# Rows of per-token scales from a repeated statistics column times the identity, in place of a row of ones times a diagonal built on VectorE (a two-block transformer kernel, one Trainium2 core)

## The reference, cut to what matters

```
def rmsnorm_2(x, g):            # mean over the features of one token
    x * rsqrt(mean(x * x, -1) + 1e-6) * g

x = x + parallel_mixer(rmsnorm_2(x, norm_mix_g), ...)
    # inside: q_a = rmsnorm_2(c_q) @ w_uq;  kv = rmsnorm_2(c_kv) @ w_ukv
    #         norms of q_nope, q_rope, k_nope for each of 4 heads, of k_rope once
x = x + memory_cross_attention(rmsnorm_2(x, norm_x_g), ...)
    # inside: norms of q and k for each of 4 heads
x = x + square(relu(rmsnorm_2(x, norm_ffn_g) @ w_ff1)) @ w_ff2
```

## Time and profile before

| | us |
|---|---|
| median of three runs | 2190.63 |
| lowest, highest | 2187.43, 2197.18 |
| the profiled execution | 2182.91 |
| its span, first to last instruction | 2181.2 |
| PE busy | 2037.4 (93%) |
| POOL busy | 1546.2 (71%) |
| DVE busy | 903.0 (41%) |
| ACT busy | 648.0 (30%) |
| mean granted clock of TensorE | 0.962 of full |

### The profile page before, as it was taken

How to read it: one execution, slowest core, us unless ns; L and a number is a source line. 1 busy time by engine, 2 the same in 40 slices (tenths; PEclk the granted TensorE clock), 3 DMA queues, 4 the chain that set the end, 5 groups by cost and what they waited for, 6 DMA issues and landing times.

```text
span 2181.2 us, 26391 instructions
## 1 busy us (share of the span) xinstructions
PE 2037.4 (93%) x9749; PEld 1625.4 (75%) x9749; DVE 903.0 (41%) x1708; ACT 648.0 (30%) x1208; POOL 1546.2 (71%) x1379
## 2 busy tenths in 40 slices
PE   6999999999999999979999997888798989999998
PEld 4888888877766667758888885866466867888887
DVE  4566666631013334355104316854645056401421
ACT  3466666551034461122002102342231132200200
POOL 6799988887644347778889877633518908988984
PEclk9999999999989999989999998988798989999999
DMA  6212211123312122313322331111102302332332
GB/s 209 78 58 61 75 59 58 59 63 111 111 46 58 54 62 78 116 59 96 97 90 91 96 99 41 46 62 58 39 1 66 109 20 78 96 96 82 98 97 72
DMA packets 212122, 165.97 MB, mean 76 GB/s; under 512 B 13439, under 2 KB 208322, under 8 KB 211635
## 3 DMA queue, kind: packets, MB, share of 16 engines
q1 hardware_dynamic: 207126, 147.61, 22.6%
q10 hardware_dynamic: 4892, 17.01, 2.3%
HBM read 161.43 MB, written 7.37 MB: 77 GB/s over the span
## 4 chain that ended last, share of the span: by engine, by line
PE 79%; POOL 10%; DVE 7%; issue 2%; ACT 2%; DMA 0%; DVEq 0%; SPq 0%; ACTq 0%; POOLq 0%
PE bank L394 59%; POOL w_lo L2519 4%; PE bank L414 4%; PE bank L1315 3%; POOL w_hi L2514 3%; PE bank L1339 2%; PE bank L1325 2%; PE bank L2075 1%; POOL x_features L652 1%; PE bank L2084 1%; POOL arena L1032 1%; PE bank L1014 1%; DVE arena L1757 1%; PE bank L992 1%; PE bank L460 1%
## 5 line engine op out<-in xcount | busy, mean ns | idle before, releaser
L2514 POOL TENSOR_TENSOR w_hi<-w_raw,one 128x512 fp32r<-128x512 f32 (+2 forms) x520 | 529.4, 1048 | 561.1 <-PE bank L394 497.0
L2519 POOL TENSOR_TENSOR w_lo<-w_raw,w_hi 128x512 fp32r<-128x512 f32 (+2 forms) x600 | 745.5, 1273 | 34.7 <-ACT w_hi L1177 30.3
L394 PE MATMUL bank<-h_hi,w_hi 128*128 128x512 f32 (+1 forms) x1144 | 461.0, 403 | 38.3 <-DVE h_lo L623 15.2
L394 PE MATMUL bank<-h_hi,w_lo 128*128 128x512 f32 (+1 forms) x1144 | 446.8, 391 | 0.0
L394 PE MATMUL bank<-h_lo,w_hi 128*128 128x512 f32 (+1 forms) x1144 | 446.3, 390 | 0.0
L394 PE MATMUL bank<-a_hi,w_hi 128*128 128x512 f32 x896 | 358.1, 400 | 11.9 <-POOL w_lo L2519 7.4
L394 PE MATMUL bank<-a_lo,w_hi 128*128 128x512 f32 x896 | 357.2, 399 | 0.0
L394 PE MATMUL bank<-a_hi,w_lo 128*128 128x512 f32 x896 | 356.7, 398 | 0.0
L394 PEld LDWEIGHTS bank<-h_hi,w_hi 128*128 128x128 f32 x1144 | 220.3, 193 | 97.0 <-issue 19.8
L394 PEld LDWEIGHTS bank<-h_hi,w_lo 128*128 128x128 f32 x1144 | 220.0, 192 | 44.9
L394 PEld LDWEIGHTS bank<-h_lo,w_hi 128*128 128x128 f32 x1144 | 220.8, 193 | 38.7 <-issue 0.2
(11 more groups left out here) (379 smaller groups left out, 2732.1 us busy)
## 6 DMA issues: line engine op xcount, KB each, us to landing
w_raw<-in_w_in SPq DMA_DIRECT2D x32, 1024.0 KB, 5.2
w_raw<-in_w_ff SPq DMA_DIRECT2D x32, 1024.0 KB, 5.5
w_raw<-in_w_mlp_in SPq DMA_DIRECT2D x16, 1024.0 KB, 5.3
w_raw<-in_w_mlp_out SPq DMA_DIRECT2D x16, 1024.0 KB, 5.9
w_raw<-in_w_in SPq DMA_DIRECT2D x25, 512.0 KB, 4.1
w_raw<-in_w_ssd_out SPq DMA_DIRECT2D x8, 1024.0 KB, 5.8
bias_rows<-bias_row ACTq DMA_DIRECT2D x1, 4096.0 KB, 16.0
w_raw<-in_w_attn_out SPq DMA_DIRECT2D x4, 1024.0 KB, 5.2
```

The lines of the kernel that those rows point to most:

```text
L394: mm = pe.matmul(bank[:, 0:ntok], a, b[:, koff + k, 0:ntok], start=(k == 0 and n == 0), stop=(k == L.kb - 1 and n == 2))
L2514: pool.tensor_tensor(w_hi[:, slot, part], raw[:, slot, part], one[:].broadcast_to([P, n]), ALU.mult).then_inc(split_hi, 1)
L2519: ins = pool.tensor_tensor(w_lo[:, slot, part], raw[:, slot, part], w_hi[:, slot, part].bitcast(F32), ALU.subtract)
```

## The change

The diagonal is no longer made. The stationary operand of the row product becomes one column of the statistics table, repeated 128 times by a zero step; the moving operand becomes the identity. One such product yields the row of one tile of 128 tokens, so a row of 512 tokens takes four products, each with a stationary operand of its own, where there was one product with 512 columns. PE now waits for the reciprocal (`nx_inverse`, `la["inverse"]`). The ring of two diagonal buffers and DVE's wait for it are gone; the ring of three PSUM banks stays. `nstat` and `lstat` hold the same numbers as before.

```diff
         def root_row_pe(pe):
-            pe.wait_ge(nx_diag, nx_n["sum"])
-            pe.matmul(NROW[:], ones[:], NROOT, start=True, stop=True).then_inc(nx_row, 1)
+            pe.wait_ge(nx_inverse, nx_n["sum"])
+            for t in range(T):
+                mm = pe.matmul(NROW[:, t * P:(t + 1) * P], nstat[:, t:t + 1].broadcast_to([P, P]), ident[:], start=True, stop=True)
+            mm.then_inc(nx_row, 1)
...
             dve.wait_ge(nx_root, nx_n["rooted"])
-            dve_link(dve.reciprocal(nstat, nstat))
+            dve.reciprocal(nstat, nstat).then_inc(nx_inverse, 1)
             row_dve(dve)
...
         def row_dve(dve):
-            n = nx_n["acc"] // DB
-            dve.tensor_tensor(NROOT.rearrange("p (t f) -> p t f", t=T), ident[:].unsqueeze(1).broadcast_to([P, T, P]),
-                              nstat.unsqueeze(2).broadcast_to([P, T, P]), ALU.mult).then_inc(nx_diag, 1)
-            dve.wait_ge(nx_row, n)
+            dve.wait_ge(nx_row, nx_n["acc"] // DB)
...
         def rows_pe(pe, n, tiles=T):
 
-            pe.wait_ge(la["diag"], n + 1)
+            pe.wait_ge(la["inverse"], 1 if n == 0 else 2 if n < 3 else 3 if n < LATENT_ITEMS else 4)
             if n >= 3:
                 pe.wait_ge(la["out"], n - 2)
-            pe.matmul(ROW_RING[n % 3][:, 0:tiles * P], ones[:], DIAG[n % 2][:, 0:tiles * P], start=True, stop=True).then_inc(la["row"], 1)
-
-        def diag_dve(dve, n, col, tiles=T):
-            if n >= 2:
-                dve.wait_ge(la["row"], n - 1)
-            r = lstat[:, col:col + tiles].unsqueeze(2).broadcast_to([P, tiles, P])
-            dve.tensor_tensor(DIAG[n % 2][:, 0:tiles * P].rearrange("p (t f) -> p t f", t=tiles),
-                              ident[:].unsqueeze(1).broadcast_to([P, tiles, P]), r, ALU.mult).then_inc(la["diag"], 1)
+            col = 4 * n if n < LATENT_ITEMS else CROSS_ITEMS[n - LATENT_ITEMS][0]
+            for t in range(tiles):
+                mm = pe.matmul(ROW_RING[n % 3][:, t * P:(t + 1) * P], lstat[:, col + t:col + t + 1].broadcast_to([P, P]), ident[:],
+                               start=True, stop=True)
+            mm.then_inc(la["row"], 1)
...
         def norms_dve(dve, first, last):
             outs = norm_outputs()
-            diag_dve(dve, first, 4 * first)
             for n in range(first, last):
-                if n + 1 < last:
-                    diag_dve(dve, n + 1, 4 * (n + 1))
                 scale_dve(dve, n, *outs[n])
...
             dve.wait_ge(la["root"], 2)
-            dve_link(dve.reciprocal(lstat[:, 4:12], lstat[:, 4:12]))
+            dve.reciprocal(lstat[:, 4:12], lstat[:, 4:12]).then_inc(la["inverse"], 1)
             norms_dve(dve, 1, 3)
```

More of the change, by code:

```diff
@@ L526, in build_program @@
         nx_sq, nx_acc, nx_sum, nx_root, nx_hi, nx_lo, nx_add = (sem(f"nx_{k}") for k in ("sq", "acc", "sum", "root", "hi", "lo", "add"))
-        NSQ, NACC, NROOT = [A(8192, 512), A(8704, 512)], A(9216, 512), A(9728, 512)
-        nx_diag, nx_row, nx_post = sem("nx_diag"), sem("nx_row"), sem("nx_post")
+        NSQ, NACC = [A(8192, 512), A(8704, 512)], A(9216, 512)
+        nx_inverse, nx_row, nx_post = sem("nx_diag"), sem("nx_row"), sem("nx_post")
         nstat, NROW = small[:, 104:104 + T], banks[5]
@@ L2002, in build_program @@
         DIAG = [t[:, 15, :] for t in (a_free_hi, a_free_lo)]
-        la = {k: sem("la_" + k) for k in ("rope", "sw", "v", "vt", "vl", "ang", "sin", "sq", "ev", "sum", "root", "diag", "row", "out", "fin", "cos", "turned")}
+        la = {k: sem("la_" + k) for k in ("rope", "sw", "v", "vt", "vl", "ang", "sin", "sq", "ev", "sum", "root", "inverse", "row", "out", "fin", "cos", "turned")}
         RR = slice(64, 128)
@@ L2249, in latent_dve @@
             dve.wait_ge(la["root"], 1)
-            dve_link(dve.reciprocal(lstat[:, 0:4], lstat[:, 0:4]))
+            dve.reciprocal(lstat[:, 0:4], lstat[:, 0:4]).then_inc(la["inverse"], 1)
             norms_dve(dve, 0, 1)
@@ L2279, in latent_dve @@
             dve.wait_ge(la["root"], 3)
-            dve_link(dve.reciprocal(lstat[:, 12:60], lstat[:, 12:60]))
+            dve.reciprocal(lstat[:, 12:60], lstat[:, 12:60]).then_inc(la["inverse"], 1)
             norms_dve(dve, 3, 7)
@@ L2391, in cross_act @@
                 kvx_act(act, b)
-            act.wait_ge(nx_diag, nx_n["root"])
+            act.wait_ge(nx_inverse, nx_n["root"])
             for h in range(X_HEADS):
@@ L2415, in cross_dve @@
             dve.wait_ge(la["root"], 4)
-            dve_link(dve.reciprocal(lstat[:, 0:cross_cols], lstat[:, 0:cross_cols]))
+            dve.reciprocal(lstat[:, 0:cross_cols], lstat[:, 0:cross_cols]).then_inc(la["inverse"], 1)
             outs = [(XK[:, h, :], colv("xk")) for h in range(X_HEADS)] + [(XQ[:, h, :], colv("xq")) for h in range(X_HEADS)]
[L2418 to L2422, removed]
+            for i, out_ in enumerate(outs):
+                scale_dve(dve, LATENT_ITEMS + i, [out_], tiles=CROSS_ITEMS[i][1])
             dve.drain().then_inc(xa_q, 1)
```

## The result

The changed kernel takes 2170.76 us in the median of nine runs (2163.85 to 2176.89), the kernel before 2189.81 in nine (2181.13 to 2197.18). The ratio is 0.9919, with a 95% interval of 0.9899 to 0.9939: faster by 0.8%, which is 17.7 us (13.4 to 22.1); the medians lie 19.1 apart. The forecast was 25.5 us. The profiled execution took 2163.85 us with a span of 2162.1, against 2182.91 and 2181.2.

The account below looks back on a forecast made before the run. The chain lay 79% on TensorE, so DVE's diagonals counted only where it crossed them, in three stretches of the second block. Six terms summed to -25.5 us, from 2190.6 to 2165 us, range 2157 to 2182.

Parts of the forecast that it names:

- Items 1 and 2: Before latent block 4: both DVE diagonals go and the block starts earlier, -7.2 us.
- The clock behind it: Latent blocks 4 and 5 with their sums run at full clock instead of 1.2 GHz, -4.8 us.
- The rival by which the clock doesn't come back: PE's clock stays low in the latent blocks and items 3 to 14; sum about -16, 2174 us; chance 0.25.
- Items 3 to 14: Rows before the latent attention: PE sets the pace, POOL's rope is late next, first rope product comes earlier, -10.1 us.
- All of it reaches the end: From the latent attention on, POOL waits for PE before splitting, so the whole -25.5 us shortens the kernel.
- term 2: Latent blocks 4 and 5: PE's shorter idle time leaves its clock up, -4.8 us.
- Cross attention: 48 row passes after the cross reciprocal let the scores start earlier, -2.3 us.
- POOL's splits beside a diagonal: After the mixer, after the MLP and at `norm_x`, POOL's splits run faster without a diagonal beside them, -1.3 us.
- Rows between panels: Six rows, item 0 and five large norms, take 0.89 us instead of 0.86 each, +0.2 us.
- slower rival: Every row product pays its weight loads, 0.19 us on each pass; +15.7 us, 2206; chance 0.04.
- three signs of error: Passes of 0.2 us or more at full clock, latent blocks at 1.2 GHz, or the attention's first product waiting for POOL.
- term 3: Items 3 to 14 before the latent attention: first rope product at 1572.8 instead of 1582.89, -10.1 us.

Follow-up runs that it names:

- e1: Kernel before with the new rows for items 1 and 2 alone; ratio 0.9942, 11.8 us below before.
- e12: Changed kernel with items 3 to 14 put back on DVE's diagonals; ratio 0.9921 to the kernel before, 16.9 us below it.
- e3: Changed kernel with 13 unread products filling TensorE's wait for POOL's rope before the attention; ratio 0.9870 to the kernel before, 29.6 us below it.
- e4: Changed kernel with POOL's rope ahead of its split of the output panel's second half; ratio 0.9853 to the kernel before, 30.8 us below it.
- e5: The changed kernel run again, nothing altered; ratio 0.9935 to the kernel before, 15.2 us below it.
- e7: Kernel before with new rows only for the cross attention, the six large norms and item 0; ratio 0.9991, 3.7 us below before.
- e8: Changed kernel with POOL's rope first and sixteen unread products ahead of items 3 to 14; ratio 0.9890 to the kernel before, 26.0 us below it.
- e9: Changed kernel with 6 unread products in TensorE's wait before the attention; ratio 0.9934 to the kernel before, 15.4 us below it.
- e11: Changed kernel with POOL's rope ahead of its split of the output panel's second half, run again; ratio 0.9861 to the kernel before, 31.6 us below it.
- e2: Kernel before with the new rows for items 3 to 14 alone; ratio 0.9982, 4.1 us below before.
- e10: Changed kernel with POOL's rope first and DVE's key rope moved ahead of the last query block; ratio 0.9885 to the kernel before, 27.0 us below it.

## Why the prediction was right, and where not

**Items 1 and 2 (-7.2).** Right: -7.0. On the time scale from the second reciprocal, block 4 moves from 12.91 to 5.91. e1 shows it alone.

**The clock behind it (-4.8).** Right: -4.4, as A falls by 11.4 in all (11.3 in e1). The rival by which the clock doesn't come back was refuted here, and came true elsewhere.

**Items 3 to 14 (-10.1).** This is the step that failed. Its own numbers held: the passes in 12.85 us (forecast 12.9), POOL's rope as what is late next, the first rope product 16.9 us after the reciprocal (forecast 16.7). It failed in what followed: "All of it reaches the end". The sum took the attention's length as given. It named POOL's rope as what is late next, and its own times leave PE 3.2 us of idle time there (1569.6 to 1572.8; 3.11 measured). It didn't ask what that does to PE's clock, though term 2 rests on that very effect. The runs put in its place +9.5 for the attention at 1.2 GHz: net -0.3 in the profiled pair, +0.9 by e12.

**Cross attention (-2.3).** Right: 11.75 to 9.41.

**POOL's splits beside a diagonal (-1.3).** Right. After the mixer 5.33 to 4.90; after the MLP the pieces take 4.93 in place of 5.38; in the `norm_x` split the three pieces on the chain take 3.70 in place of 4.14.

**Rows between panels (+0.2).** About right: item 0's eight passes take 0.89 us, where the earlier trace rows have 0.86.

```profile
1486.91 0.89 PE bank L2085 x8
```

**The sum.** -7.0 - 4.4 - 0.3 - 2.3 - 1.3 is -15.3, beside measured medians of -19.1 (0.9919) and -15.2 (0.9935), whose intervals both hold it. The spans of the profiled pair differ by 19.1, along the program: 5.5 ahead of the second reciprocal, 11.7 in A, B and C, 1.9 the other way up to the cross reciprocal, 2.3 up to the scores and 1.5 behind them. Of the first 5.5 the change can account for 0.9 (POOL's pieces after the mixer and the MLP). 3.8 arise between 1424 and 1469, where PE's clock differs (0.67 against 0.91 between 1440 and 1460). That looks like chance: in the other executions with the same code up to there (e3, e4, e5, and e7 to e12) the second reciprocal stands anywhere from 1502.65 to 1507.43. The 1.9 are mainly the 96 panel products at 1697.40, 1.5 us slower (last section). The 1.5 behind the scores are unexplained.

**The slower rival** (weight loads not hidden) is refuted: a pass costs 0.11 us at 2.4 GHz (8 in 0.89, 16 in 1.80), and its load, 0.227 in the mean, doesn't show. The estimate of 0.64 us more for a row, worked out from the page of the Trainium skill named in the prediction, isn't seen: 0.89 us for eight passes, where 0.86 was the price of the one product before. What the Trainium skill says in the same section ("TensorE: Matmul & The Clock Gate", "Step-by-step: what each phase is for"), that PE pulls loads ahead of matmuls in flight, fits that better.

**What the prediction asked to be shown** came, and so did one of its three signs of error, that the attention's first product waits for POOL. As a sign it contradicts term 3, whose own times have that product wait for POOL.

**Luck.** That the median lies inside the range owes something to it. The 9.5 us lost in the attention stand in no term and no rival. The range had room for them only because it allowed for 10.5 us of misses in two other clock terms (0 for -4.8, -4.4 for -10.1), which did not come. And the median of -19.1 is 4 us nearer to the forecast of -25.5 than what the parts account for.

## What to carry to other kernels

When a change makes TensorE early for something it didn't wait for before, price the wait twice: its length, and what runs at half the clock behind it. Here 3.1 us cost 9.5 more, and moving another engine's order, or filling the gap with unread products, brought it back. Look at the whole gap, not at its end: here filling begun after the clock had gone paid nothing (e8), and nor did half a filling (e9). And an operation with two SBUF inputs on DVE is priced by what GpSimd does beside it, 0.68 to 4.9 us for the same instruction.

## What was not expected of the hardware

**A gap of the same length falls on either side.** Four executions kept the clock over 1.70 or 1.71 us of idle time, and one lost it after 1.63, before the same product. Counted from the third reciprocal, the gap of e9 began 1.5 to 1.8 us later, behind work of the same kind. No run here tells what decides.

**A faster TensorE loses its clock at the next wait.** Behind `norm_x` the last panels of 256 memory tokens are paced by POOL's split, and 96 panel products of 512 tokens follow. Before the change PE ran the first at a mean clock of 0.91 (1695 to 1714), was still at work until 1713.05, waited 1.4 us, and then took 22.76 us for the 96. The changed kernel ran them at the full clock, waited longer, and lost the clock for it. Its window of PE over the first:

```profile
1680.00:1697.00 17.00, 11.57 (x95) 1.00 0.38 123
```

the group with the first product behind the wait (busy us, mean ns, idle us before it and what ended it):

```profile
L394 PE MATMUL bank<-a_hi,w_hi 128*128 128x512 f32 x1 | 0.8, 794 | 2.9 <-POOL w_lo L2509 2.9
```

and the windows of the fall:

```profile
1697.00:1698.00 1.00, 0.60 (x2) 0.70 0.00 0
1698.00:1701.00 3.00, 3.00 (x9) 0.53 0.85 244
```

24.28 us for the 96: being faster cost 1.5. In e11 the same panels of 256 ran at 0.81, the wait was 0.34 us, and the 96 took 22.75. e1, e2, e5, e9 and e10 (24.28 to 24.30) are like the changed kernel; e4, e7, e8 and e12 (22.75 or 22.76) like e11. So it isn't the change that decides: such a stretch moves by 1.5 us with where the clock happens to stand on entering it, which is more than some terms of the sum, and it is about half of why e10's earlier start is not seen at its end.

**At the attention the fall comes behind the wait, elsewhere in it.** In after, PE ran for 1.7 us at 2.4 GHz between the end of its wait and the fall, in e9 for 2.0, in e2 for 0.9, and e3 shows that the cause stands ahead of all that. But in the kernel before the clock fell at 1512 with PE idle, and in after between 1533 and 1534, in the 1.18 us of idle time ahead of the last sums.
